# Attention in split halves: three single-pass matmuls for each full-precision f32 matmul of the scores and values

## Chip, cores and metric

One core of a Trainium2 chip runs the whole kernel. The metric is the device time of one execution, the median of three runs. TensorE (PE) multiplies, ScalarE (ACT) and VectorE (DVE) do the elementwise work, SyncE (SP) issues nearly all DMAs.

## What is computed

One layer of a bidirectional encoder over 256 tokens of width 2048: a SwiGLU feed-forward block (5632 wide), a mixing block, a second feed-forward block and a final RMS norm. The mixing block runs a 31-tap depthwise convolution and a latent attention on the same normalised input, gates both with sigmoids and projects the sum. The attention is what the change touches:

```
c_q  = rms_norm(c_q_raw)                      # 768 wide
q    = c_q @ w_uq    -> 16 heads x (128 nope + 64 rope)
c_kv = rms_norm(c_kv_raw)                     # 512 wide
k_nope, v = c_kv @ w_ukv -> 16 heads x (128, 128)
q_rope, k_rope = rotated by the positions     # one k_rope for all heads
s = q_nope . k_nope + q_rope . k_rope
p = softmax(s * 192 ** -0.5)
o = p @ v ;  y_mla = o @ w_o
```

All inputs and outputs are float32.

## The kernel before

**Units.** All weights stream through four slots. A unit is two 128-row blocks of 512 columns (1024 elements a partition), or a smaller one; there are some 814 units, numbered by u over the whole program. SyncE loads unit u into `raw` when VectorE has done with unit u - 4. ScalarE's `round_unit(u)` copies it to `w_hi` as fp32r, once TensorE has used unit u - 4; VectorE's `split_unit(u)` subtracts, `w_lo = raw - w_hi`. The activations are kept in high and low fp32r halves in the same way. `multiply` then makes three single-pass matmuls, high by high, high by low and low by high, into one PSUM bank. ScalarE and VectorE run a loop over u each, four units ahead of TensorE, and whatever else they do stands in that loop at fixed places, so that their order is written out by hand.

**The stages** in order: ffn1 up and down, the convolution's inputs, the latents, the two gates, the rotary queries (`q_rope`), the heads (units H0 = 422 to 453), mla_out (from M0 = 454), conv_out, w_out, ffn2.

**The heads.** Four units for each of eight head pairs s: two of queries (768 elements), one of keys, one of values (1024). `head_pair(s)` on TensorE is: scores of pair s - 1, first query unit (18 matmuls of 256 columns), values of pair s - 2, second query unit (18), keys (24), values' projection (24), then eight 128x128 transposes of the probabilities of pair s - 1 (`attend_turn`). The scores of pair 7 and the values of 6 and 7 stand among the first units of mla_out. Scores and values are matmuls of plain f32 operands, `q_nope`, `k_nope`, `q_rope`, `k_rope`, `probs_t` and `value`.

On ScalarE and VectorE, s is (u - H0) // 4 - 1 and part is (u - H0) % 4. In order within a unit, before the change:
- part 0: ScalarE `attend_exp` of pair s - 1 (waits for the row maximum), the unit, taps, `attend_scale`; VectorE `attend_max`, the unit, taps, `attend_inv`.
- part 1: ScalarE the unit, taps, `attend_out` of pair s - 2 (high half of the head output); VectorE the unit, taps, `keep_queries`, `split_heads`.
- part 2: ScalarE the unit, taps, `keep_keys`; VectorE the unit and taps.
- part 3: ScalarE the unit, taps, `keep_values`, `attend_turn` of pair s - 1 (two copies of turned probabilities); VectorE the unit and taps.

**Taps.** The convolution's 4 x 31 taps, each on four channel blocks, run beside the matmuls. Two of three are four multiplications on ScalarE (`make_tap`, L565) and one addition on VectorE a unit later (`take_tap`, L1185); the third kind is four multiply-adds on VectorE (L1191). `taps_due(u)` says how many are due at unit u: 0.85 a unit up to the rotary queries, after which 110 are done, and then from unit H0 + 4 one a unit until the last 14, which are taps 17 to 30 of the last channel group. `attend_out` of pair 4 waits for the last tap. The convolution's working buffers share memory with the rotary queries and the head outputs; the trace calls all of it q_rope.

**Lines that the prediction speaks of:** L457 `round_unit`, L995 `split_unit`, L565, L1185 and L1191 taps, L572 exponentials, L581 scaling, L588 copies of turned probabilities, L595 and L1218 head outputs, L601 and L607 keys and values, L1212 queries, L1197 row maximum, L1206 reciprocals, L866 and L867 scores, L892 values, L877 transposes, L727 to L729 `multiply`.

Of the kernel before, what the change touches and what calls it, by code (L numbers as in the profile page):

```python
# [14 lines left out]
P = 128  # L15
# [46 lines left out]
class Turn:  # L62


    def __init__(self, hi_before, lo_before, hi, lo):
# [6 lines left out]
         "qrope": (2, 1, 0), "merge": (2, 1, 1)}  # L72
# [6 lines left out]
class Plan:  # L79
    def __init__(self):  # L80
# [14 lines left out]
        self.k_turn = self.more_turns(1, 2, 0)  # L95
# [11 lines left out]
        self.probs_turn = self.more_turns(2 * PAIRS, 1, 0)  # L107
# [56 lines left out]
def encoder(nc, streams, xt_in, x_in, pos_in, gains_in, final_in, taps_in, const_in, freq_in, out):  # L164
# [6 lines left out]
    with ExitStack() as ctx:  # L171
# [10 lines left out]
        h = sb("h", [P, KT, 2, T], F32R)  # L182
# [24 lines left out]
        probs_t = sb("probs_t", [P, 2, 2 * T], F32, outs)  # L207
# [33 lines left out]
        q_rope = sb("q_rope", [P, PAIRS, 4, T], F32, outs)  # L241
        outs.close()
        conv_acc = q_rope[:, 4:8, 1, :]
        conv_prod = (q_rope[:, 4:8, 2, :], q_rope[:, 4:8, 3, :])
# [15 lines left out]
        k_rope = sb("k_rope", [P, 2, T])  # L260
        q_nope = sb("q_nope", [P, 2, T])
        k_nope = sb("k_nope", [P, 2, T])
        value = sb("value", [P, 2, 2, 2 * P])
# [54 lines left out]
        query_step = sem("query_step")  # L318
        q_copied = sem("q_copied")
# [130 lines left out]
        def _(act):  # L450
# [58 lines left out]
            def take_turns(n):  # L509

                g = groups[n]
                for b in range(g.turns):
# [4 lines left out]
                    if g.kind in ("up", "merge"):  # L517
                        dst = hidden if g.kind == "up" else merged
# [8 lines left out]
                    elif g.kind == "qrope":  # L527
                        act.activation(q_rope[:, k:k + 2, 0, :], pair, ACT.Copy).then_inc(turn_hi, 1)

            def take_late_turns():  # L530
# [8 lines left out]
                for j in range(2):  # L539
                    rows = slice(ROPE * j, ROPE * (j + 1))  # L540
                    act.activation(k_rope[rows, j, :], t[rows, 0:T], ACT.Copy).then_inc(turn_hi, 1)
# [54 lines left out]

            def keep_keys(s):
# [40 lines left out]
            for u in range(n_units):  # L638
# [83 lines left out]
        def _(pe):  # L722
# [130 lines left out]
            def attend_scores(p):  # L853
# [3 lines left out]
                pe.wait_ge(turn_hi, turns[g.turn + p % 4 // 2].hi_before + 1)  # L857
# [586 lines left out]
```

## Time and profile before

| | us |
|---|---|
| median of three runs | 2320.63 (2319.89 to 2320.98) |
| the profiled execution, its whole time | 2320.78 |
| its span | 2318.6 |

| engine | busy us | share | instructions |
|---|---|---|---|
| TensorE matmul | 2298.7 | 99% | 10718 |
| TensorE weight load | 1924.2 | 83% | 10718 |
| VectorE | 1322.5 | 57% | 1473 |
| ScalarE | 1188.1 | 51% | 1621 |

The span is what the profiler saw between the first and the last instruction; the execution's own time is 2.2 us more. TensorE's granted clock is 0.999 of full. A matmul row's duration covers a pipelined instruction, so the pace is read from one start to the next. An instruction of ScalarE or VectorE overlaps the next one a little in the same way. L numbers are lines of the kernel before.

### The profile page before, as it was taken

Reading aid. Unit: us, or ns where it says so; the run is one execution under the profiler, and the core shown is the slowest. Engines: PE = TensorE matmul, PEld = TensorE weight load, DVE = VectorE, ACT = ScalarE, POOL = GpSimd, SP = SyncE. Lnnn points to the kernel's source line nnn. Section 1 sums busy time; section 2 is a strip of 40 time slices with the busy share of each in tenths; the row PEclk is TensorE's granted clock in tenths of the full one; section 3 lists DMA queues with packets and bytes.
Section 4 is the critical chain, followed back from the end, with each engine's and each line's share of the span. In section 5 each row is a group of like instructions: output and inputs, shape, how many; then the busy total and the mean of one; then the engine's idle time right before and its main releaser. Section 6 shows DMA issues by size and latency. Waiting matters only on the chain.

```text
span 2318.6 us, 26793 instructions
## 1 busy us (share of the span) xinstructions
PE 2298.7 (99%) x10718; PEld 1924.2 (83%) x10718; DVE 1322.5 (57%) x1473; ACT 1188.1 (51%) x1621; POOL 0.2 (0%) x4
## 2 busy tenths in 40 slices
PE   8999999999999999999999999999999999999998
PEld 7888888888888888878899888888888888888887
DVE  5444544544545488997875465555544554544444
ACT  6444444444444577787776564445444444444443
POOL 0000000000000000000000000000000000000000
PEclk9999999999999999999999999999999999999999
DMA  8666666666666666566643456556666666666664
GB/s 290 190 189 192 189 185 195 190 186 190 192 190 189 191 191 183 180 192 186 200 135 115 139 176 185 183 182 213 190 186 190 190 190 190 190 186 195 192 192 154
DMA packets 121309, 432.65 MB, mean 187 GB/s; under 512 B 13665, under 2 KB 13921, under 8 KB 121057
## 3 DMA queue, kind: packets, MB, share of 16 engines
q1 hardware_dynamic: 121040, 430.51, 60.6%
q8 instruction: 85, 1.39, 0.3%
q10 hardware_dynamic: 144, 0.43, 0.0%
q14 instruction: 40, 0.32, 0.0%
HBM read 428.78 MB, written 2.10 MB: 186 GB/s over the span
## 4 chain that ended last, share of the span: by engine, by line
PE 97%; DVE 1%; ACT 1%; issue 1%; DMA 0%; SPq 0%; ACTq 0%; DVEq 0%
PE bank L727 31%; PE bank L729 31%; PE bank L728 31%; PE turned L738 2%; PE bank L892 1%; PE bank L866 1%; PE bank L867 1%; DVE q_rope L1185 0%; DMA raw<-in_ffn_up 0%; PE turned L877 0%; ACT w_hi L457 0%; DVE w_lo L995 0%; DVE q_rope L1191 0%; PE turned L946 0%; ACT q_rope L565 0%
## 5 line engine op out<-in xcount | busy, mean ns | idle before, releaser
L995 DVE TENSOR_TENSOR w_lo<-raw,w_hi 128x1024 fp32r<-128x1024 f32 (+1 forms) x813 | 985.7, 1215 | 955.2 <-ACT w_hi L457 954.9
L457 ACT ACTIVATE w_hi<-raw 128x1024 fp32r<-128x1024 f32 (+1 forms) x813 | 852.0, 1051 | 997.8 <-PE bank L729 982.4
L727 PE MATMUL bank<-w_hi,h 128*128 128x512 f32 (+1 forms) x2144 | 835.7, 390 | 9.6 <-DVE w_lo L1255 6.4
L729 PE MATMUL bank<-w_hi,h 128*128 128x512 f32 (+1 forms) x2144 | 832.6, 388 | 0.0
L728 PE MATMUL bank<-w_lo,h 128*128 128x512 f32 (+1 forms) x2144 | 832.5, 388 | 0.0
L727 PEld LDWEIGHTS bank<-w_hi,h 128*128 128x128 f32 x2144 | 403.1, 188 | 92.6 <-DVE w_lo L1255 6.4
L729 PEld LDWEIGHTS bank<-w_hi,h 128*128 128x128 f32 x2144 | 402.9, 188 | 82.9
L728 PEld LDWEIGHTS bank<-w_lo,h 128*128 128x128 f32 x2144 | 403.0, 188 | 81.3
L727 PE MATMUL bank<-w_hi,hidden 128*128 128x512 f32 x704 | 274.3, 390 | 0.0
L729 PE MATMUL bank<-w_hi,hidden 128*128 128x512 f32 x704 | 273.9, 389 | 0.0
L728 PE MATMUL bank<-w_lo,hidden 128*128 128x512 f32 x704 | 273.9, 389 | 0.0
L729 PEld LDWEIGHTS bank<-w_hi,hidden 128*128 128x128 f32 x704 | 132.2, 188 | 27.5
L728 PEld LDWEIGHTS bank<-w_lo,hidden 128*128 128x128 f32 x704 | 132.2, 188 | 27.4
L727 PEld LDWEIGHTS bank<-w_hi,hidden 128*128 128x128 f32 x704 | 132.2, 188 | 27.1
L565 ACT ACTIVATE q_rope<-padded,taps 128x256 f32<-128x256 f32 x320 | 135.6, 497 | 1.0 <-DVE q_rope L1185 1.0
L1185 DVE TENSOR_TENSOR q_rope<-q_rope 128x1024 f32<-128x1024 f32 x76 | 92.6, 1218 | 0.0
L1191 DVE SCALAR_TENSOR_TENSOR q_rope<-padded,taps,q_rope 128x256 f32<-128x256 f32 x160 | 66.7, 479 | 0.0
L484 ACT ACTIVATE opened<-bank,rstd 128x512 f32<-128x512 f32 x52 | 32.9, 684 | 37.4 <-PE bank L729 37.4
L727 PE MATMUL bank<-w_hi,attn 128*128 128x512 f32 x128 | 52.0, 406 | 0.0
L727 PE MATMUL bank<-w_hi,merged 128*128 128x512 f32 x128 | 50.2, 392 | 0.0
L729 PE MATMUL bank<-w_hi,attn 128*128 128x512 f32 x128 | 50.1, 391 | 0.0
L728 PE MATMUL bank<-w_lo,attn 128*128 128x512 f32 x128 | 49.9, 390 | 0.0
(184 smaller groups left out, 1226.7 us busy)
## 6 DMA issues: line engine op xcount, KB each, us to landing
raw<-in_ffn_up SPq DMA_DIRECT2D x351, 512.0 KB, 4.1
raw<-in_ffn_down SPq DMA_DIRECT2D x176, 512.0 KB, 3.7
raw<-in_conv_in SPq DMA_DIRECT2D x64, 512.0 KB, 4.1
raw<-in_conv_gate SPq DMA_DIRECT2D x32, 512.0 KB, 4.3
raw<-in_mla_gate SPq DMA_DIRECT2D x32, 512.0 KB, 4.0
raw<-in_mla_out SPq DMA_DIRECT2D x32, 512.0 KB, 3.6
raw<-in_conv_out SPq DMA_DIRECT2D x32, 512.0 KB, 3.6
raw<-in_w_out SPq DMA_DIRECT2D x32, 512.0 KB, 3.6
```

The lines of the kernel that those rows point to most:

```text
L457: act.activation(w_hi[:, j, 0:n], raw[:, j, 0:n], ACT.Copy).then_inc(hi_ready, 1)
L484: act.activation(opened[:, tt, :], banks(g)[tt][:, :], func, scale=rstd[:, tt:tt + 1]).then_inc(by_act, 1)
L565: act.activation(conv_prod[made % 2][:, r, :], padded[:, m, t:t + T], ACT.Copy, scale=taps[:, m, t:t + 1]).then_inc(tap_made, 1)
L727: pe.matmul(dst, fixed_hi, moving_hi, start=first, stop=False)
L728: pe.matmul(dst, fixed_hi, moving_lo, start=False, stop=False)
L729: return pe.matmul(dst, fixed_lo, moving_hi, start=False, stop=last)
L738: last = pe.transpose(turned_bank[n % 2][:, r * T + tt * P:r * T + (tt + 1) * P], src[:, tt, c:c + P], identity[:, :])
L866: pe.matmul(dst, q_nope[:, j, cols], k_nope[:, j, :], start=True, stop=False)
L867: last = pe.matmul(dst, q_rope[:, p, 0, cols], k_rope[:, j, :], start=False, stop=True)
L995: dve.tensor_tensor(w_lo[:, j, 0:n], raw[:, j, 0:n], w_hi[:, j, 0:n], ALU.subtract).then_inc(lo_ready, 1)
L1185: dve.tensor_tensor(dst, conv_acc, conv_prod[made % 2], ALU.add).then_inc(tap_done, 1)
L1191: dve.scalar_tensor_tensor(out=conv_acc[:, r, :], in0=padded[:, m, t:t + T], scalar=taps[:, m, t:t + 1], in1=conv_acc[:, r, :], op0=ALU.mu ...
```

## The change

- `q_nope`, `k_nope`, `q_rope` and `k_rope` get a low half beside the high one and become fp32r; `probs_t` and `value` become fp32r and get `probs_lo` and `value_lo` beside them. The rotary queries and the new low halves lie where `h` lies, which is not in use then.
- Each f32 matmul of scores and values becomes a `multiply` of three fp32r matmuls.
- ScalarE makes all high halves: the query copy moves to it from VectorE (part 1, after `attend_out`).
- VectorE makes the low halves by subtraction: queries (part 1), keys (part 2), values and then the two of the probabilities (part 3), each time after the unit and its tap; also those of the rotary queries and the rotary key in the stages ahead.
- TensorE waits for the low halves (`q_copied`, `k_copied`, `v_copied` and `turn_lo` now count them).
- After unit H0 + 4 the taps are due at 0.65 a unit in place of 1.

```diff
@@ -69,7 +69,7 @@
-         "qrope": (2, 1, 0), "merge": (2, 1, 1)}
+         "qrope": (2, 1, 1), "merge": (2, 1, 1)}
@@ -104,7 +104,7 @@
-        self.probs_turn = self.more_turns(2 * PAIRS, 1, 0)
+        self.probs_turn = self.more_turns(2 * PAIRS, 1, 1)
@@ -385,7 +397,7 @@
         def taps_due(u):
-            n = int(0.85 * max(0, min(u, QR0) - CONV0)) + max(0, u - H0 - 4)
+            n = int(0.85 * max(0, min(u, QR0) - CONV0)) + int(0.65 * max(0, u - H0 - 4))
             open_groups = sum(u >= g.last + 7 for g in plan.stage("conv_in") if g.kind == "glu")
             return min(n, TAPS * open_groups, N_TAPS)
@@ -594,18 +604,23 @@
                 for j in range(2):
                     act.activation(attn[:, 2 * p + j, 0, :], out_bank[:, j * T:(j + 1) * T], ACT.Copy).then_inc(head_hi, 1)
+            def keep_queries(s):
+                act.wait_ge(unit_used, H0 + 4 * s + 2)
+                if s:
+                    act.wait_ge(scores_ready, 2 * s)
+                act.activation(q_nope[:, :, 0, :], q_bank[:, :].rearrange("p (j t) -> p j t", j=2), ACT.Copy).then_inc(q_hi, 1)
+
             def keep_keys(s):
                 act.wait_ge(unit_used, H0 + 4 * s + 3)
                 if s:
                     act.wait_ge(scores_ready, 2 * s)
-                act.activation(k_nope[:, :, :].rearrange("p j t -> p (j t)"), k_bank[:, :], ACT.Copy).then_inc(k_copied, 1)
+                act.activation(k_nope[:, :, 0, :], k_bank[:, :].rearrange("p (j t) -> p j t", j=2), ACT.Copy).then_inc(k_hi, 1)
             def keep_values(s):
                 act.wait_ge(unit_used, H0 + 4 * s + 4)
                 if s > 1:
                     act.wait_ge(value_summed, s - 1)
-                act.activation(value[:, s % 2, :, :].rearrange("p k d -> p (k d)"), v_bank[:, :],
-                               ACT.Copy).then_inc(v_copied, 1)
+                act.activation(value[:, s % 2, :, :].rearrange("p k d -> p (k d)"), v_bank[:, :], ACT.Copy).then_inc(v_hi, 1)
             def fore(n):
                 i, tt = n // 2, n % 2
@@ -681,6 +696,8 @@
                     attend_scale(s - 1)
                 if (s == PAIRS + 1 and part == 0) or (2 <= s <= PAIRS and part == 1):
                     attend_out(s - 2)
+                if part == 1 and 0 <= s < PAIRS:
+                    keep_queries(s)
                 if part == 2 and 0 <= s < PAIRS:
                     keep_keys(s)
                 if part == 3 and 0 <= s < PAIRS:
@@ -854,7 +871,7 @@
                 pe.wait_ge(q_copied, p + 1)
                 pe.wait_ge(k_copied, p + 1)
                 g = plan.stage("q_rope")[p // 4]
-                pe.wait_ge(turn_hi, turns[g.turn + p % 4 // 2].hi_before + 1)
+                pe.wait_ge(turn_lo, turns[g.turn + p % 4 // 2].lo_before + 1)
                 if p:
                     pe.wait_ge(exp_ready, 4 * p)
                 else:
@@ -863,8 +880,10 @@
                     for q in range(2):
                         cols = slice(q * P, (q + 1) * P)
                         dst = scores[j][:, q * T:(q + 1) * T]
-                        pe.matmul(dst, q_nope[:, j, cols], k_nope[:, j, :], start=True, stop=False)
-                        last = pe.matmul(dst, q_rope[:, p, 0, cols], k_rope[:, j, :], start=False, stop=True)
+                        multiply(dst, (q_nope[:, j, 0, cols], q_nope[:, j, 1, cols]),
+                                 (k_nope[:, j, 0, :], k_nope[:, j, 1, :]), True, False)
+                        last = multiply(dst, (q_rope[:, p, 0, cols], q_rope[:, p, 1, cols]),
+                                        (k_rope[:, j, 0, :], k_rope[:, j, 1, :]), False, True)
                     last.then_inc(scores_ready, 1)
             def attend_turn(p):
@@ -886,11 +905,13 @@
                 else:
                     pe.wait_ge(*freed(groups[plan.first_mla - 1]))
                 t = turns[plan.probs_turn + 2 * p + 1]
-                pe.wait_ge(turn_hi, t.hi_before + 1)
+                pe.wait_ge(turn_lo, t.lo_before + 1)
                 for j in range(2):
                     for k in range(2):
-                        last = pe.matmul(out_bank[:, j * T:(j + 1) * T], value[:, p % 2, k, j * P:(j + 1) * P],
-                                         probs_t[:, j, k * T:(k + 1) * T], start=(k == 0), stop=(k == 1))
+                        dims, keys = slice(j * P, (j + 1) * P), slice(k * T, (k + 1) * T)
+                        last = multiply(out_bank[:, j * T:(j + 1) * T],
+                                        (value[:, p % 2, k, dims], value_lo[:, p % 2, k, dims]),
+                                        (probs_t[:, j, keys], probs_lo[:, j, keys]), k == 0, k == 1)
                 last.then_inc(value_summed, 1)
             def block_of(u, k):
@@ -1206,11 +1232,26 @@
                     dve.reciprocal(row_inv[:, j, :], row_sum[:, j, :]).then_inc(inv_ready, 1)
             def keep_queries(s):
-                dve.wait_ge(unit_used, H0 + 4 * s + 2)
-                if s:
-                    dve.wait_ge(scores_ready, 2 * s)
-                dve.tensor_scalar(q_nope[:, :, :].rearrange("p j t -> p (j t)"), q_bank[:, :], 1.0, None,
-                                  ALU.mult).then_inc(q_copied, 1)
+                dve.wait_ge(q_hi, s + 1)
+                dve.tensor_tensor(q_nope[:, :, 1, :], q_bank[:, :].rearrange("p (j t) -> p j t", j=2), q_nope[:, :, 0, :],
+                                  ALU.subtract).then_inc(q_copied, 1)
+
+            def keep_keys(s):
+                dve.wait_ge(k_hi, s + 1)
+                dve.tensor_tensor(k_nope[:, :, 1, :], k_bank[:, :].rearrange("p (j t) -> p j t", j=2), k_nope[:, :, 0, :],
+                                  ALU.subtract).then_inc(k_copied, 1)
+
+            def keep_values(s):
+                dve.wait_ge(v_hi, s + 1)
+                hi, lo = (v[:, s % 2, :, :].rearrange("p k d -> p (k d)") for v in (value, value_lo))
+                dve.tensor_tensor(lo, v_bank[:, :], hi, ALU.subtract).then_inc(v_copied, 1)
+
+            def attend_turn(p):
+                for j in range(2):
+                    n = plan.probs_turn + 2 * p + j
+                    dve.wait_ge(turn_hi, turns[n].hi_before + 1)
+                    dve.tensor_tensor(probs_lo[:, j, :], turned_bank[n % 2][:, :], probs_t[:, j, :],
+                                      ALU.subtract).then_inc(turn_lo, 1)
             def split_heads(p):
                 dve.wait_ge(head_hi, 2 * p + 2)
@@ -1302,6 +1343,12 @@
                     keep_queries(s)
                 if (s == PAIRS + 1 and part == 0) or (2 <= s <= PAIRS and part == 1):
                     split_heads(s - 2)
+                if part == 2 and 0 <= s < PAIRS:
+                    keep_keys(s)
+                if part == 3 and 0 <= s < PAIRS:
+                    keep_values(s)
+                if part == 3 and 1 <= s <= PAIRS:
+                    attend_turn(s - 1)
                 if u == FORE + AHEAD + 8:
                     mean_of_channels()
                 if u == FORE + AHEAD + 11:
...
```

## Rows read from the trace of the kernel before

**Rows 1.** The page, part 1: busy time, share and instructions of each engine.
```profile
PE 2298.7 (99%) x10718; PEld 1924.2 (83%) x10718; DVE 1322.5 (57%) x1473; ACT 1188.1 (51%) x1621; POOL 0.2 (0%) x4
```

**Rows 2.** Stretches, scores to scores: length, busy PE PEld DVE ACT POOL, clock, DMA share, GB/s.
```profile
core 0: us, PE busy (x) PEld busy (x) DVE busy (x) ACT busy (x) POOL busy (x), PEclk, DMA share, GB/s
1184.57:1200.07 15.50, 14.60 (x111) 13.97 (x109) 10.53 (x18) 14.24 (x32) 0.00 (x0) 1.00 0.37 113
1200.07:1218.10 18.03, 16.34 (x117) 15.51 (x117) 13.57 (x25) 14.25 (x35) 0.00 (x0) 1.00 0.36 110
...
1234.44:1250.56 16.12, 16.12 (x118) 15.50 (x117) 8.54 (x15) 10.06 (x23) 0.00 (x0) 1.00 0.40 118
```

**Rows 3.** Timeline of PE, 1215 to 1225: start, us, engine, line, instruction, tiles, shape, idle before.
```profile
1215.38 1.04 PE L877 MATMUL turned<-identity,probs 128*128 128x128 f32 x8
...
1218.10 0.67 PE L866 MATMUL bank<-k_nope,q_nope 128*128 128x256 f32 x2 [1.69 <-issue]
...
1218.61 0.59 PE L867 MATMUL bank<-k_rope,q_rope 128*128 128x256 f32 x2
...
1219.04 0.59 PE L866 MATMUL bank<-k_nope,q_nope 128*128 128x256 f32 x2
...
1221.75 0.28 PE L728 MATMUL bank<-c_q,w_hi 128*128 128x256 f32 x1
...
1221.87 0.28 PE L729 MATMUL bank<-c_q,w_lo 128*128 128x256 f32 x1
...
1223.78 1.89 PE L892 MATMUL bank<-probs_t,value 128*128 128x256 f32 x8
```

**Rows 4.** Timeline of ACT, 1214 to 1229, same columns.
```profile
1214.35 0.63 ACT L595 ACTIVATE attn<-bank 128x256 fp32r<-128x256 f32 x2
...
1214.87 1.05 ACT L457 ACTIVATE w_hi<-raw 128x1024 fp32r<-128x1024 f32 x1
...
1215.83 1.70 ACT L565 ACTIVATE q_rope<-padded,taps 128x256 f32<-128x256 f32 x4
...
1217.42 0.58 ACT L601 ACTIVATE k_nope<-bank 128x512 f32<-128x512 f32 x1
...
1218.84 0.59 ACT L607 ACTIVATE value<-bank 128x512 f32<-128x512 f32 x1
...
1219.32 1.07 ACT L588 ACTIVATE probs_t<-turned 128x512 f32<-128x512 f32 x2
...
1222.18 0.47 ACT L572 ACTIVATE probs<-bank,row_max 128x256 f32<-128x256 f32 x1 [1.79 <-DVE row_max L1200]
...
1224.04 0.84 ACT L457 ACTIVATE w_hi<-raw 128x768 fp32r<-128x768 f32 x1
...
1227.56 1.71 ACT L581 ACTIVATE probs<-probs,row_inv 128x256 f32<-128x256 f32 x4 [1.09 <-DVE row_inv L1206]
```

**Rows 5.** Timeline of DVE, 1215 to 1228, same columns.
```profile
1215.33 0.68 DVE L1212 TENSOR_SCALAR q_nope<-bank 128x512 f32<-128x512 f32 x1
...
1215.93 0.74 DVE L1218 TENSOR_TENSOR attn<-bank,attn 128x256 fp32r<-128x256 f32 x2
...
1216.60 1.21 DVE L995 TENSOR_TENSOR w_lo<-raw,w_hi 128x1024 fp32r<-128x1024 f32 x1
...
1217.73 1.22 DVE L1185 TENSOR_TENSOR q_rope<-q_rope 128x1024 f32<-128x1024 f32 x1
...
1221.26 0.68 DVE L1197 TENSOR_REDUCE row_inv<-bank 128x2 f32<-128x512 f32 x1
...
1225.79 1.67 DVE L1191 SCALAR_TENSOR_TENSOR q_rope<-padded,taps,q_rope 128x256 f32<-128x256 f32 x4
...
1227.37 0.22 DVE L1206 RECIPROCAL row_inv<-row_sum 128x2 f32<-128x2 f32 x2
```

**Rows 6.** Instructions of line L1127: count, ns min/median/max, first and last start, shape.
```profile
L1127 DVE TENSOR_TENSOR hidden<-turned,hidden x44: 679/681/684, 61.3 to 2079.0; 128x512 fp32r<-128x512 f32 x44
```

**Rows 7.** Timeline of PE at the very start of the execution.
```profile
6.42 0.79 PE L727 MATMUL bank<-w_hi,h 128*128 128x512 f32 x1 [6.42 <-DVE w_lo L1255]
...
9.58 0.63 PE L728 MATMUL bank<-w_lo,h 128*128 128x512 f32 x1
```

More of the change, by code:

```diff
@@ L181, in encoder @@
         x = sb("x", [P, 2, D])
-        h = sb("h", [P, KT, 2, T], F32R)
+        outs = ExitStack()
+        h = sb("h", [P, KT, 2, T], F32R, outs)
+        outs.close()
+        outs = ExitStack()
+        q_rope = sb("q_rope", [P, PAIRS, 2, T], F32R, outs)
+        q_nope = sb("q_nope", [P, 2, 2, T], F32R, outs)
+        k_nope = sb("k_nope", [P, 2, 2, T], F32R, outs)
+        probs_lo = sb("probs_lo", [P, 2, 2 * T], F32R, outs)
+        value_lo = sb("value_lo", [P, 2, 2, 2 * P], F32R, outs)
+        outs.close()
+        sb("place_of_h", [P, KT, 2, T], F32R)
         identity = sb("identity", [P, P])
@@ L240, in encoder @@
         outs = ExitStack()
-        q_rope = sb("q_rope", [P, PAIRS, 4, T], F32, outs)
+        scratch = sb("scratch", [P, PAIRS, 4, T], F32, outs)
         outs.close()
-        conv_acc = q_rope[:, 4:8, 1, :]
-        conv_prod = (q_rope[:, 4:8, 2, :], q_rope[:, 4:8, 3, :])
+        conv_acc = scratch[:, 4:8, 1, :]
+        conv_prod = (scratch[:, 4:8, 2, :], scratch[:, 4:8, 3, :])
         merged = sb("merged", [P, KT, 2, T], F32R)
@@ L259, in encoder @@
         c_q = sb("c_q", [P, QT, 2, T], F32R)
[L260 to L263, printed above, removed]
+        k_rope = sb("k_rope", [P, 2, 2, T], F32R)
+        value = sb("value", [P, 2, 2, 2 * P], F32R)
         gain = {}
@@ L318, in encoder @@
         query_step = sem("query_step")
+        q_hi = sem("q_hi")
+        k_hi = sem("k_hi")
+        v_hi = sem("v_hi")
         q_copied = sem("q_copied")
@@ L516, in take_turns @@
                     k = 2 * b + (0 if g.kind in ("kv", "q1") else 4 * g.i)
-                    if g.kind in ("up", "merge"):
-                        dst = hidden if g.kind == "up" else merged
+                    if g.kind in ("up", "merge", "qrope"):
+                        dst = {"up": hidden, "merge": merged, "qrope": q_rope}[g.kind]
                         act.activation(dst[:, k:k + 2, 0, :], pair, ACT.Copy).then_inc(turn_hi, 1)
@@ L540, in take_late_turns @@
                     rows = slice(ROPE * j, ROPE * (j + 1))
-                    act.activation(k_rope[rows, j, :], t[rows, 0:T], ACT.Copy).then_inc(turn_hi, 1)
+                    act.activation(k_rope[rows, j, 0, :], t[rows, 0:T], ACT.Copy).then_inc(turn_hi, 1)
             def make_tap(n):
@@ L1123, in take_turns @@
                     k = 2 * b + (0 if g.kind in ("kv", "q1") else 4 * g.i)
-                    if g.kind in ("up", "merge"):
-                        dst = hidden if g.kind == "up" else merged
+                    if g.kind in ("up", "merge", "qrope"):
+                        dst = {"up": hidden, "merge": merged, "qrope": q_rope}[g.kind]
                         dve.wait_ge(turn_hi, t.hi_before + 1)
@@ L1142, in take_late_turns @@
                                              op1=ALU.subtract).then_inc(turn_lo, 1)
+                dve.wait_ge(turn_hi, turns[plan.k_turn].hi_before + 2)
+                for j in range(2):
+                    rows = slice(ROPE * j, ROPE * (j + 1))
+                    dve.tensor_tensor(k_rope[rows, j, 1, :], turned_bank[plan.k_turn % 2][rows, 0:T], k_rope[rows, j, 0, :],
+                                      ALU.subtract).then_inc(turn_lo, 1)
             def clear_once():
@@ L1208, in keep_queries @@
             def keep_queries(s):
-                dve.wait_ge(unit_used, H0 + 4 * s + 2)
-                if s:
-                    dve.wait_ge(scores_ready, 2 * s)
-                dve.tensor_scalar(q_nope[:, :, :].rearrange("p j t -> p (j t)"), q_bank[:, :], 1.0, None,
-                                  ALU.mult).then_inc(q_copied, 1)
+                dve.wait_ge(q_hi, s + 1)
[10 more added lines that the diff above has]
+            def attend_turn(p):
+                for j in range(2):
+                    n = plan.probs_turn + 2 * p + j
+                    dve.wait_ge(turn_hi, turns[n].hi_before + 1)
+                    dve.tensor_tensor(probs_lo[:, j, :], turned_bank[n % 2][:, :], probs_t[:, j, :],
+                                      ALU.subtract).then_inc(turn_lo, 1)
             def split_heads(p):
```

10 lines of the change are left out of this document (4 added, 6 removed).

## The prediction

> **What bounds the kernel now.** I read the page first [rows 1]: TensorE is busy 99% of the span and is nearly the whole of the chain that ended last, at a full granted clock. So a microsecond taken from its queue is a microsecond of the end, as long as no other engine makes it wait for longer. Then the stretches between one head pair's scores and the next [rows 2], because the change touches only the attention of the eight head pairs. TensorE's own work for a pair is 84 projection matmuls of 256 columns at 0.12 us from start to start, the scores, the values and eight transposes (0.87). A quiet stretch is just that, 16.12 us; the two that carry convolution taps are 15.50 (a pair without values, whose work is 14.41) and 18.03, so they hold stalls of 1.09 and 1.89. Then the three queues in the second of these [rows 3 to 5]: TensorE finishes its transposes at 1216.25 and starts the scores at 1218.10. The page puts that gap down to "issue", but the ScalarE row beside it says what ended it: the copy of k_nope, started at 1217.42 behind a tap of 1.70 us, ended at 1218.00. So in this part of the kernel ScalarE and VectorE already sit at TensorE's heels, and the tap work decides.
>
> **What TensorE saves.** Every f32 matmul shows as two instructions, 0.433 us for the pair (1218.61 to 1219.04, [rows 3]), or 0.216 each. A head pair has 8 such matmuls in the scores (3.46 us) and 4 in the values (1.73 us; the row with x8). Afterwards each is three fp32r matmuls of 256 columns. The nearest rows are the projections around them: same shape, fp32r on both sides, 1221.75 to 1221.87, so 0.12 us each including the weight load. I take it: scores 24 x 0.12 = 2.88, values 12 x 0.12 = 1.44, so 0.87 us less for a pair, 6.95 for eight. TensorE's own work of a stretch becomes 15.27 (13.83 for the first).
>
> **What the two others get.** ScalarE gets a copy of the queries (it takes over the high half that VectorE copied): a 128x512 copy out of a bank, 0.58 us, 0.48 from start to start (1218.84 to 1219.32, [rows 4]). VectorE gives up its query copy (0.60 from start to start, 1215.33 to 1215.93, [rows 5]) and gets five subtractions of 128x512: queries, keys, values and two of probabilities. No such row stands in this stage, but the same form is there elsewhere, 0.681 us each [rows 6]; I take 0.60 as its step, like the copy of the same size, since other 0.68 rows of VectorE follow each other at 0.60. The bounds are 0.55 and 0.67. That is 4 x 0.60 = 2.4 us more for VectorE in a pair. The taps are thinned from 1 to 0.65 for a unit, so the 14 that are left at this point are done over 22 units in place of 14 (taps 17 to 30 of the last channel group): ScalarE makes ten of them (1.60 each), VectorE adds these ten (1.14 each) and makes the other four itself (1.58 each). The tap work itself is not less, and it now reaches into pair 5.
> More important is where the new work stands: the scores now wait for the keys' low half, that is for ScalarE's copy and then VectorE's subtraction, each behind that engine's conversion of the next weight unit, its tap and whatever else its queue holds. And VectorE does the low halves of values and probabilities (0.60 + 1.20) ahead of the row maximum, on which the exponentials wait, with ScalarE's later work behind them.
>
> **The walk.** I went through the three queues in program order, each operation starting when its engine is free and what it waits for has arrived. Steps in us from start to start, all from [rows 3 to 5]: ScalarE conversion 0.96 (128x1024; done at 1.06) and 0.74 (128x768; done at 0.85), tap 1.60, copy 0.48 (done at 0.58), exponential 0.45 with its accumulator read, four scalings 1.62, head copies 0.52; VectorE subtraction of a unit 1.13 or 0.87, tap 1.14 or 1.58, maximum with its scaling 0.80 (the first is through at 0.87), low half 0.60 (done at 0.69), head low halves 0.67, reciprocals 0.2; 0.06 us from a semaphore to the next start, 0.16 from TensorE's next start to its event. Walked through the old program, this starts the scores at 1184.5, 1200.07, 1218.24 and so on to 1298.96, with 3.15 us of stalls; the trace has 1200.07 and 1218.10, and 2.98 of stalls. So it carries the old kernel to within 0.2 us.
> Without taps the new chain from one pair's scores to the next one's is hidden. VectorE reaches the maximum at 2.78 (what is left of the keys' step is -0.15 of overlap, then unit 1.13, values 0.60, probabilities 1.20); first exponential at 3.71, four of them to 5.51; conversion done and seen 0.91, its subtraction 0.87, reciprocals seen 0.28: scaling from 7.57 to 9.19; conversion 0.74, head copies 0.52, queries' high half seen 0.64; the keys' weight unit then waits for TensorE (11.74), its conversion is seen at 12.86, subtracted at 13.99, and the keys' low half is seen at 14.74, before the 15.27 at which TensorE arrives. Half a microsecond is spare, and a tap on either queue costs more than that.
> With taps, the worst stretch (pair 4 to pair 5): the maximum at -0.15 + 1.13 + tap 1.58 + 0.60 + 1.20 = 4.36; first exponential +0.93, exponentials +1.80, conversion +0.91, unit +0.87, tap +1.14, reciprocals +0.28: scaling starts at 10.29; +1.62, conversion +0.74, tap +1.60, head copies +0.52, queries' high half +0.64 = 15.41; VectorE: queries' low +0.60, heads +0.67, unit +1.13, tap +1.14, keys' low +0.75 = 19.70. TensorE's own work is 15.27, so it waits 4.43. In the same way: pair 0 waits 2.03 (VectorE still has the queries' rotary turns and tap 17 ahead of the keys), 0 to 1 is 15.92 against 13.83 (2.09), 1 to 2 is 18.10 (2.83), 2 to 3 is 18.26 (2.99), 3 to 4 is 16.40 (1.13), 5 to 6 is hidden, 6 to 7 is 15.68 (0.41), and the last values wait 0.22. Together 16.1 us of stalls.
>
> **Sum.** Stalls 16.1 - 3.15 = +13.0; TensorE's work -6.95; together +6.0 us. The rest costs nothing: the rotary keys' two low halves (64 rows each) and the larger clearing fall into stages in which TensorE has no stall after them, and the DMAs are at 0.36 to 0.40 of their time in these stretches [rows 2]. The profiled execution took 2320.78 (span 2318.6), 0.15 above the median of 2320.63, so the sum goes on the median: 2326.6. With the low half's step at 0.55 the walk gives +4.5, at 0.67 +8.1; with 0.03 or 0.10 us for a semaphore +5.4 or +6.8.
>
> **Rivals.**
> A, faster: the low halves hide. The two stalls of before came from taps in front of the keys; thinning the taps alone takes the walk's 3.15 to 0.9. If VectorE's subtractions found room, the gain would be 6.95 + 2.3 = 9.2, so 2311.4. The point at which it turns is a stall total of 10.1 us (6.95 + 3.15). For it: VectorE is busy only 8.5 of 16.12 us in a quiet stretch [rows 2]. Against: it is not the load but the order; in the stretch of 18.03 it is busy 13.6, and adding to a queue on whose end TensorE waits can't be free.
> B, no change to be told: the queues run a little closer than my steps and the stalls come to some 12 us: +1.9, so 2322.5. For it: the walk adds eight small overruns of one sign.
> C, the clock: TensorE's rows at the very start stand 0.43 us apart after 6.42 us of idleness, where they are 0.23 later: half pace, the lower of its two levels (1.2 against 2.4 GHz), for the 3.6 us up to 10.0 [rows 7]. The old stalls, at most 1.9 us, were granted 1.00 on both sides. The new one of 4.4 us is longer than any within the old kernel. If the clock falls there once, that costs half of 3.6 us, 1.8: 2328.4; in the three stretches around 3 us too, 2333.8.
> The Trainium skill has this as a rule ("TensorE: Matmul & The Clock Gate", section "HAM oscillation — how this bites in real kernels"): an engine that stands idle between bursts of matmuls falls back to its half rate and starts the next burst cold. The start of this trace agrees; the gaps inside the old kernel don't show it.
> D, the replaced matmuls are not single passes: were they at the 0.216 of the f32 halves, 36 a pair would take 8 x 36 x 0.096 = 28 us more than I reckon, and fill some 8 of the stalls' 16 us: 2346. The projections' rows speak against it.
>
> **How the numbers follow.** Forecast (+4.5 to +8.1) 0.58, A 0.08, B 0.18, C 0.14, D 0.02. About 0.2%, 4.6 us, is what can be told from no change here. Faster is A, 0.08; same is B and the lowest of the forecast's own band, 0.20; slower is the rest, 0.72. The range leaves out A, D and C's upper end: 2321.5 to 2330.5.
>
> **What would show it.** In the trace of after: score matmuls 0.12 us apart; gaps in front of the scores of pairs 0 to 5, the longest at pair 5, each ended by VectorE's subtraction into k_nope; no gap at pair 6; the row maximum behind the probabilities' subtractions; stretches of 15.3 in the quiet end against 18 to 20 with taps; taps that end in pair 5. Wrong it would be if the gaps summed to less than 10 us (A), or if matmuls behind the longest gap stood at double their distance (C). If the keys' low half is not what the scores wait for, the walk has named the wrong chain even where the total fits.

## The result, and the profile after

| | kernel before | changed kernel |
|---|---|---|
| median of seven runs, us | 2320.18 (2319.89 to 2320.98) | 2328.36 (2327.80 to 2330.21) |
| span of the profiled execution, us | 2318.6 | 2326.1 |
| ratio of the times | | 1.0036, 95% interval 1.0027 to 1.0045 |

The changed kernel is 0.36% slower, 8.2 us by the medians and 7.5 by the two spans. Its page, parts 1 and 4 (against [rows 1]):

```profile
PE 2297.4 (99%) x10814; PEld 1925.8 (83%) x10814; DVE 1343.9 (58%) x1511; ACT 1190.8 (51%) x1629; POOL 0.2 (0%) x4
PE 94%; DVE 3%; ACT 2%; issue 1%; DMA 0%; SPq 0%; ACTq 0%
```

TensorE's busy time fell by only 1.3 us, and it lost three points of the chain that ended last (its share fell from 97% to 94%), two of them to VectorE and one to ScalarE. The stretches from one pair's scores to the next one's answer to [rows 2], with the same columns:

```profile
core 0: us, PE busy (x) PEld busy (x) DVE busy (x) ACT busy (x) POOL busy (x), PEclk, DMA share, GB/s
1186.47:1202.38 15.91, 14.06 (x117) 13.86 (x117) 10.46 (x19) 13.38 (x30) 0.00 (x0) 1.00 0.31 109
1202.38:1220.59 18.21, 16.98 (x128) 16.77 (x129) 13.45 (x24) 13.54 (x32) 0.00 (x0) 0.91 0.40 119
1220.59:1238.78 18.19, 15.47 (x128) 15.26 (x129) 13.36 (x24) 13.19 (x32) 0.00 (x0) 1.00 0.32 98
1238.78:1255.02 16.24, 15.48 (x128) 15.28 (x129) 11.78 (x20) 11.30 (x28) 0.00 (x0) 1.00 0.29 100
1255.02:1274.58 19.56, 15.48 (x128) 15.27 (x129) 13.44 (x24) 14.13 (x33) 0.00 (x0) 1.00 0.33 106
1274.58:1291.30 16.72, 16.72 (x129) 16.72 (x129) 9.69 (x17) 8.48 (x20) 0.00 (x0) 0.90 0.40 116
1291.30:1306.98 15.68, 15.49 (x132) 15.28 (x130) 10.13 (x17) 10.95 (x25) 0.00 (x0) 1.00 0.43 133
```

The first number after the stretch is its length, the one behind the comma TensorE's busy time. TensorE's own work is 13.83 in the first and 15.27 in the others. Each stretch is longer than that, four of them by 2 to 4.3 us, and two carry a granted clock of about 0.9. The scores of pair 0 start 1.87 us later than before. The first transpose of the convolution, which closes this part of the program, starts 7.51 later (1333.15 against 1325.64), so the whole change of the span lies in the heads.

Which step ends the longest gap, the one in front of pair 5, is seen when VectorE's and ScalarE's timelines are laid side by side. VectorE, 1255 to 1275, with the idle time before an operation in brackets:

```profile
1255.97 1.67 DVE L1217 SCALAR_TENSOR_TENSOR scratch<-padded,taps,scratch 128x256 f32<-128x256 f32 x4
1257.55 0.68 DVE L1247 TENSOR_TENSOR value_lo<-bank,value 128x512 fp32r<-128x512 f32 x1
1258.15 1.28 DVE L1253 TENSOR_TENSOR probs_lo<-turned,probs_t 128x512 fp32r<-128x512 f32 x2
1259.35 0.68 DVE L1223 TENSOR_REDUCE row_inv<-bank 128x2 f32<-128x512 f32 x1
...
1263.84 1.22 DVE L1211 TENSOR_TENSOR scratch<-scratch 128x1024 f32<-128x1024 f32 x1
1264.97 0.22 DVE L1232 RECIPROCAL row_inv<-row_sum 128x2 f32<-128x2 f32 x2
...
1270.26 0.69 DVE L1236 TENSOR_TENSOR q_nope<-bank,q_nope 128x512 fp32r<-128x512 f32 x1 [1.66 <-ACT q_nope L611]
1270.87 0.74 DVE L1259 TENSOR_TENSOR attn<-bank,attn 128x256 fp32r<-128x256 f32 x2
1271.53 1.21 DVE L1016 TENSOR_TENSOR w_lo<-raw,w_hi 128x1024 fp32r<-128x1024 f32 x1
1272.66 1.22 DVE L1211 TENSOR_TENSOR padded<-scratch 128x1024 f32<-128x1024 f32 x1
1273.80 0.68 DVE L1241 TENSOR_TENSOR k_nope<-bank,k_nope 128x512 fp32r<-128x512 f32 x1
```

ScalarE in the same stretch:

```profile
1265.17 1.71 ACT L591 ACTIVATE probs<-probs,row_inv 128x256 f32<-128x256 f32 x4 [2.24 <-DVE row_inv L1232]
1266.78 0.83 ACT L469 ACTIVATE w_hi<-raw 128x768 fp32r<-128x768 f32 x1
1267.52 1.70 ACT L575 ACTIVATE scratch<-padded,taps 128x256 f32<-128x256 f32 x4
1269.12 0.63 ACT L605 ACTIVATE attn<-bank 128x256 fp32r<-128x256 f32 x2
1269.65 0.58 ACT L611 ACTIVATE q_nope<-bank 128x512 fp32r<-128x512 f32 x1
```

Read in order of time, this is the chain. On VectorE a tap and the low halves of values and probabilities stand ahead of the row maximum (1259.35), and another tap stands ahead of the reciprocals (1264.97). On ScalarE a tap and the head copies stand ahead of the queries' high half (1269.65). On VectorE a weight unit and a tap stand ahead of the keys' low half, which ends at 1274.48. TensorE, which had finished its transposes, starts the scores 0.10 us later:

```profile
1269.47 1.04 PE L896 MATMUL turned<-identity,probs 128*128 128x128 f32 x8
1274.58 0.36 PE L744 MATMUL bank<-k_nope,q_nope 128*128 128x256 f32 x1 [4.08 <-issue]
...
1275.83 0.41 PE L745 MATMUL bank<-k_nope,q_nope 128*128 128x256 f32 x1
1276.05 0.41 PE L746 MATMUL bank<-k_nope,q_nope 128*128 128x256 f32 x1
...
1278.66 0.28 PE L744 MATMUL bank<-k_rope,q_rope 128*128 128x256 f32 x1
1278.78 0.28 PE L745 MATMUL bank<-k_rope,q_rope 128*128 128x256 f32 x1
```

"issue" again stands for a wait that the page can't name; the end of L1241 beside it does. The same distance of 0.10 us lies between the end of L1241 and the scores of pairs 0 to 4 (for pair 1, 1202.28 and 1202.38). And behind this gap the matmuls stand 0.22 us apart (1275.83 to 1276.05), three microseconds later 0.12: TensorE ran at its lower level for a while. The granted clock in 4 us behind the gaps of pairs 1, 3 and 5:

```profile
1202.40:1206.40 4.00, 4.00 (x22) 4.00 (x23) 4.00 (x6) 2.47 (x6) 0.00 (x0) 0.62 0.79 208
1238.78:1242.78 4.00, 4.00 (x33) 4.00 (x34) 3.97 (x7) 0.94 (x3) 0.00 (x0) 1.00 0.57 190
1274.60:1278.60 4.00, 4.00 (x21) 4.00 (x22) 3.57 (x6) 0.36 (x1) 0.00 (x0) 0.57 0.62 200
```

### The profile page after: what moved, and what is told of

Read it like the earlier page. It is cut to its first block, busy times and chain, and to the rows that moved or that the text cites. A ratio compares the mean times of both kernels' runs of the same rounds, so it can differ in the third digit from the quotient of the medians.

```text
span 2326.1 us, 27031 instructions
## 1 busy us (share of the span) xinstructions
PE 2297.4 (99%) x10814; PEld 1925.8 (83%) x10814; DVE 1343.9 (58%) x1511; ACT 1190.8 (51%) x1629; POOL 0.2 (0%) x4
## 4 chain that ended last, share of the span: by engine, by line
PE 94%; DVE 3%; ACT 2%; issue 1%; DMA 0%; SPq 0%; ACTq 0%
PE bank L744 31%; PE bank L745 31%; PE bank L746 31%; PE turned L755 2%; DVE scratch L1211 1%; DVE w_lo L1016 1%; ACT w_hi L469 1%; DVE scratch L1217 0%; ACT scratch L575 0%; ACT probs L582 0%; ACT probs L591 0%; DMA raw<-in_ffn_up 0%; DVE probs_lo L1253 0%; PE turned L967 0%; DVE q_nope L1236 0%
## 5 line engine op out<-in xcount | busy, mean ns | idle before, releaser
L1016 DVE TENSOR_TENSOR w_lo<-raw,w_hi 128x1024 fp32r<-128x1024 f32 (+1 forms) x813 | 985.5, 1215 | 942.0 <-ACT w_hi L469 941.6
L575 ACT ACTIVATE scratch<-padded,taps 128x256 f32<-128x256 f32 x320 | 135.7, 497 | 1.0 <-DVE scratch L1211 1.0
L1211 DVE TENSOR_TENSOR scratch<-scratch 128x1024 f32<-128x1024 f32 x76 | 92.5, 1218 | 0.0
L1217 DVE SCALAR_TENSOR_TENSOR scratch<-padded,taps,scratch 128x256 f32<-128x256 f32 x160 | 66.6, 478 | 0.0
```

The lines of the kernel that those rows point to most:

```text
L575: act.activation(conv_prod[made % 2][:, r, :], padded[:, m, t:t + T], ACT.Copy, scale=taps[:, m, t:t + 1]).then_inc(tap_made, 1)
L1016: dve.tensor_tensor(w_lo[:, j, 0:n], raw[:, j, 0:n], w_hi[:, j, 0:n], ALU.subtract).then_inc(lo_ready, 1)
L1211: dve.tensor_tensor(dst, conv_acc, conv_prod[made % 2], ALU.add).then_inc(tap_done, 1)
L1217: dve.scalar_tensor_tensor(out=conv_acc[:, r, :], in0=padded[:, m, t:t + T], scalar=taps[:, m, t:t + 1], in1=conv_acc[:, r, :], op0=ALU.mu ...
```

## The experiments

The theory on trial: what is lost is the wait for the chain of steps on ScalarE and VectorE between one pair's scores and the next one's; it is the taps in those two queues that push it past TensorE's 15.27 us; and a part of the loss is the clock behind long gaps. The rivals: the low halves cost by themselves, taps or not; ScalarE's added copy or the thinned taps do it; the sum of VectorE's work does it in whatever order.

All times are medians; "before" in the same sessions was 2320.16 to 2320.30. A gap is the time of a stretch less TensorE's own work in it; the idle time in brackets in a timeline is a little shorter (4.08 against a gap of 4.29 at pair 5).

| run | us | ratio to before, 95% interval |
|---|---|---|
| e1 changed, taps early | 2318.13 | 0.9992 (0.9982 to 1.0001) |
| e2 old, taps early | 2322.43 | 1.0011 (1.0002 to 1.0020) |
| e3 old, taps thin | 2318.18 | 0.9991 (0.9981 to 1.0000) |
| e4 changed, gaps filled | 2326.43 | 1.0027 (1.0017 to 1.0038) |
| e5 changed, no low halves | 2313.82 | 0.9973 (0.9962 to 0.9983) |
| e6 changed, f32 matmuls | 2331.75 | 1.0050 (1.0035 to 1.0065) |
| e7 changed, keys first | 2324.74 | 1.0019 (1.0010 to 1.0028) |
| e8 keys first, taps spread | 2315.39 | 0.9979 (0.9970 to 0.9989) |
| e9 keys first, taps eased | 2311.19 | 0.9959 (0.9944 to 0.9973) |
| e10 old, taps eased | 2316.93 | 0.9984 (0.9974 to 0.9993) |
| e11 changed, old tap rate | 2328.01 | 1.0032 (1.0021 to 1.0044) |

### e1 and e2: the taps out of the heads

```diff
-            n = int(0.85 * max(0, min(u, QR0) - CONV0)) + int(0.65 * max(0, u - H0 - 4))
+            n = int(0.85 * max(0, min(u, QR0 - 64) - CONV0)) + int(1.1 * max(0, min(u, QR0) - QR0 + 64))
```

e2 is the same edit in the kernel before.

> The changed kernel with all convolution taps done before the heads: from 64 units ahead of the rotary queries 1.1 taps a unit in place of 0.85, none in the heads. Nothing else differs. Theory (it is the taps in the queues of ScalarE and VectorE that let the new chain overrun TensorE's 15.27 us): gaps in front of the scores fall from some 14 us to about 1.5, a stretch is 15.3 everywhere, the clock stays at full pace, and the time is 8.6 under the kernel before, 2311.6. Rival (the low halves cost by themselves, taps or not): gaps of 1 to 2 us stay in front of most scores, the time stays above 2320. Second rival (the taps' work only moves): the gate stages, where VectorE is busy 31 to 37 of 40 us, get stalls instead; then the heads are as in the theory but the stretch before them is longer by some us.

> The kernel before with the same early taps. Theory: it has only the 3.0 us of stalls to lose, so about 2317.1; together with the run of the changed kernel with early taps this gives what the split halves bring without taps: 5.5 us less (6.95 of matmuls less 1.5 of gaps). Rival (low halves cost by themselves): this kernel is the faster one of the two.

Measured 2318.13 and 2322.43: the split halves now win by 4.3 us, where 5.5 were expected, but they lie 6.5 and 5.3 us above the forecasts (2311.6 and 2317.1). The heads did what the theory said: in e1 the scores are 13.81, then five times 15.25 us apart, with 0.25 us of idle time before pair 0 and 0.18 before pair 7; in e2 they are 14.40 and 16.11 apart. The second rival is right about the rest: the taps moved their price into the gate stages. TensorE's waits between 900 and 1175 in e1 (engine, line, waited for, us in total, times, longest):

```profile
PE bank L744 <- DVE w_lo L1016: 5.5, 5, 2.1
```

The kernel before has 1.9 us in three such waits there, and e2 5.3 in four. That is 3.6 and 3.4 us more. The granted clock explains a further part of what lies over the forecasts. e1, behind an idle time of 2.00 us:

```profile
988.00:992.00 4.00, 4.00 (x11) 3.17 (x12) 3.84 (x12) 3.95 (x8) 0.00 (x0) 0.57 0.45 133
```

Here 43% of 4 us is lost, 1.7 us; in e2 the clock is 0.62 in the 4 us from 1004.32 and 0.95 in the next 4, which is 1.7 too. So in the heads the low halves cost less than 1 us by themselves: from the first scores to the convolution's transposes e1 takes 131.91 us and e2 137.98, which is 6.07 of the matmuls' 6.95. Ahead of the heads they may cost something: pair 0's scores start 1.4 us later in e1 than in e2 (1191.36 and 1189.96), of which TensorE's waits show 0.5; the cause of the rest is open. VectorE has little room there even without the extra taps: in the kernel before it is busy 38.46 of the 40 us from 940 to 980.

### e3 and e11: is it the thinning?

e3 is the kernel before with 0.65 taps a unit in the heads, e11 the changed kernel with 1:

```diff
-            n = int(0.85 * max(0, min(u, QR0) - CONV0)) + max(0, u - H0 - 4)
+            n = int(0.85 * max(0, min(u, QR0) - CONV0)) + int(0.65 * max(0, u - H0 - 4))
```

> The kernel before with the changed kernel's thinning of taps alone (0.65 a unit in place of 1 in the heads). The walk through the queues gives 0.9 us of stalls in place of 3.15, so 2317.9. Rival (thinning is what costs, as it drags the taps out to pair 5): slower than before by some us, with gaps at pairs 3 to 5.

> The changed kernel with the old tap rate in the heads (1 a unit, done in pair 3, in place of 0.65, done in pair 5). Theory (it is the total of tap work between the scores' chains that counts, not how it is spread): the walk gives gaps of 3.2, 3.9, 4.0 and 4.4 us in front of pairs 0 to 3 and 16.1 us in all, the same as for the changed kernel; 5.9 us over the kernel before, 2326.1, and up to 4 more where the clock falls behind three gaps of about 4 us, 2326 to 2330. Rival (thin taps are what makes this change bearable): over 2331.

e3 took 2318.18, against 2317.9 expected: thinning is the good part of the change, worth 2 us in the old kernel, whose one remaining gap is 0.7 us. The interval just reaches 1, but the slowest of e3's ten runs (2319.32) is faster than the fastest of the kernel before (2319.70). e11 took 2328.01, the time of the changed kernel (2328.36) within its spread. Its stretches are 18.53, 19.35 and 19.80 and then 15.24: fewer, longer gaps and the same sum. Both rivals are out. Between these two rates the spread of the taps doesn't matter to the changed kernel, which fits the theory that their total in the chains does.

### e4: the gaps filled

```diff
+                fill = {1: 12, 2: 12, 3: 12, 5: 28}.get(p, 0)
+                if fill:
+                    pe.wait_ge(exp_ready, 4 * p)
+                    for _ in range(fill):
+                        pe.matmul(scores[0][:, 0:T], c_q[:, 0, 0, 0:P], c_q[:, 0, 0, :], start=True, stop=True)
                 pe.wait_ge(q_copied, p + 1)
```

> The changed kernel with idle TensorE time in front of the scores of pairs 1, 2, 3 (12 each) and 5 (28) filled by dummy 256-column fp32r matmuls into the score bank, which the scores then overwrite; nothing waits for longer. Theory (TensorE's clock falls after the long gaps and that costs about 1.5 us behind pair 5's gap): with the engine kept busy the score matmuls all stand 0.12 us apart, the granted clock is 1.00 in each stretch, and the time is about 1.3 us under the changed kernel, 2327.0. Rival (the doubled distance of some 15 matmuls after the gaps has another cause, as the weight unit's transfer or the operands' place): it stays, and the time is that of the changed kernel, 2328.4.

Measured 2326.43, 1.9 us under the changed kernel. TensorE in front of pair 5's scores, and the granted clock behind them:

```profile
1270.83 3.60 PE L875 MATMUL bank<-c_q 128*128 128x256 f32 x28
1275.16 0.35 PE L744 MATMUL bank<-k_nope,q_nope 128*128 128x256 f32 x1 [0.73 <-issue]
...
1276.06 0.28 PE L745 MATMUL bank<-k_nope,q_nope 128*128 128x256 f32 x1
1276.18 0.28 PE L746 MATMUL bank<-k_nope,q_nope 128*128 128x256 f32 x1
```

```profile
1275.00:1279.00 4.00, 3.84 (x32) 3.88 (x33) 3.96 (x8) 0.18 (x1) 0.00 (x0) 1.00 0.69 226
```

The matmuls stand 0.12 apart at a clock of 1.00, and the stretch from pair 5 to pair 6 is 15.22 in place of 16.72. Of the other stretches only pair 1 to pair 2 changed (17.97 against 18.21), so the doubled distance was the clock, and it cost 1.5 us behind pair 5's gap and 0.24 behind pair 1's. From the first scores to the convolution's transposes e4 takes 144.94 us, the changed kernel 146.68, 1.74 more.

### e5 and e6: one part alone

e5 keeps the three matmuls and drops the low halves:

```diff
-                                 (k_nope[:, j, 0, :], k_nope[:, j, 1, :]), True, False)
+                                 (k_nope[:, j, 0, :], k_nope[:, j, 0, :]), True, False)
...
-                                        (value[:, p % 2, k, dims], value_lo[:, p % 2, k, dims]),
+                                        (value[:, p % 2, k, dims], value[:, p % 2, k, dims]),
```

and so on for the other operands. e6 keeps the low halves and their waits and drops the three matmuls:

```diff
-                        multiply(dst, (q_nope[:, j, 0, cols], q_nope[:, j, 1, cols]),
-                                 (k_nope[:, j, 0, :], k_nope[:, j, 1, :]), True, False)
+                        pe.matmul(dst, q_nope[:, j, 0, cols].bitcast(F32), k_nope[:, j, 0, :].bitcast(F32), start=True, stop=False)
```

> The changed kernel without the low halves of queries, keys, values and probabilities: the three matmuls stay, with the high half in the low one's place, and TensorE waits for the high halves alone. This leaves out the attention's low-order terms and VectorE's subtractions. Theory (the loss is the wait for the low halves' chain): the walk gives 2.6 us of gaps in place of some 14 and 7.5 us less than the kernel before, 2312.7. Rival (ScalarE's added query copy and the thinned taps are what makes the scores late): the gaps stay near those of the changed kernel and the time above 2325.

> The changed kernel with all its low halves made and waited for, but one f32 matmul of the high halves in the place of the three (the low-order terms of the attention are left out). TensorE then does the old 0.87 us a pair more. Theory: part of that lies in gaps that are there anyway, so not 6.95 but 3.4 us more than the changed kernel's walk: 9.4 us over the kernel before, 2329.6, and up to 1.5 more where the clock falls behind the long gap, 2331. Rival (TensorE is the bound in all stretches): 6.95 over the changed kernel, 2335.3.

e5 took 2313.82 (expected 2312.7), 6.4 us less than before with the taps still in the heads. One gap of size is left, 1.8 us in front of pair 1 (two more are 0.3 and 0.4); a quiet stretch is 15.23. So ScalarE's query copy and the taps alone cost little, and the low halves' chain with the taps costs 2328.36 - 2313.82 = 14.5 us, the clock's share included. e6 took 2331.75 (expected 2329.6 to 2331), 3.4 us over the changed kernel where TensorE does 6.95 us more: half of the matmuls' saving falls into gaps and is worth nothing. TensorE still idles 3.38 us in front of its pair 5.

### e7: another order of the same work

```diff
                 if part == 0 and 1 <= s <= PAIRS:
                     attend_exp(s - 1)
+                if part == 2 and 0 <= s < PAIRS:
+                    keep_keys(s)
...
-                if part == 2 and 0 <= s < PAIRS:
-                    keep_keys(s)
                 if part == 3 and 0 <= s < PAIRS:
                     keep_values(s)
```

on ScalarE, and likewise on VectorE.

> The changed kernel with the keys' high and low halves put ahead of the next weight unit and of the tap on ScalarE and VectorE; no other order changes. Theory (the order in the queues decides): the gap in front of pair 0 goes, the others shrink to 1 to 2.7 us, small gaps of up to 1.7 us come in front of the values; the walk gives 13.1 us in all in place of 16.1, 3.0 us less than the changed kernel's walk, and with no gap over 2.7 us the clock should stay up at pair 5: 2323 to 2325. Rival (VectorE has too much work in all, order or not): as the changed kernel, 2328.4.

Measured 2324.74, in the range. Pair 0 starts at 1185.29 (before the edit 1186.47), and the clock is 1.00 behind its gaps. New small gaps stand where the walk had put them, in front of the values (`probs_t`), beside those that are left in front of the scores:

```profile
1217.86 0.36 PE L744 MATMUL bank<-k_nope,q_nope 128*128 128x256 f32 x1 [0.69 <-issue]
1224.69 0.35 PE L744 MATMUL bank<-probs_t,value 128*128 128x256 f32 x1 [1.56 <-DVE probs_lo L1253]
1236.05 0.36 PE L744 MATMUL bank<-k_nope,q_nope 128*128 128x256 f32 x1 [0.93 <-issue]
```

The same operations in another order cost 3.6 us less, so the sum of VectorE's work alone is not the cause. Of the 3.6, 1.3 is the stretch from pair 5 to pair 6 (15.45 in place of 16.72), which is the clock. But the order alone doesn't save the change.

### e8 to e10: a version that beats both

e8 is e7 with this tap schedule, and e9 with the next one; e10 is the kernel before with e9's.

```diff
+            n = int(1.05 * max(0, min(u, QR0 - 88) - CONV0) + 0.5 * max(0, min(u - QR0 + 88, 24)) + 1.07 * max(0, min(u, QR0) - QR0 + 64))
```

```diff
+            n = int(1.1 * max(0, min(u, QR0 - 88) - CONV0) + 0.4 * max(0, min(u - QR0 + 88, 24)) + 0.75 * max(0, min(u - QR0 + 64, 14)) + 1.06 * max(0, min(u, QR0 + 5) - QR0 + 50))
```

> The changed kernel with the keys' halves first as in the run before, and all taps before the heads, but spread by VectorE's load: 1.05 a unit in the convolution's input stage, 0.5 in the latents, 1.07 in the gates. Theory: no gaps in the heads but 0.2 us, 9.9 us less than the kernel before (2310.3) if the earlier stages take the taps without new stalls; the first try with early taps had 5.5 us of stalls between 950 and 1170, against 1.9 before, so with the lighter load in the latents something between 2310 and 2314. Rival (VectorE is too full before the heads however the taps are spread): 2317 to 2318, as with the first early taps.

> As the run with the keys first and spread taps, but the taps are eased where its profile showed the stalls: 1.1 a unit in the convolution's input stage, 0.4 in the latents, 0.75 for the first 14 gate units (in which VectorE also normalises the queries), then 1.06 up to one unit before the last rotary one. Theory: no gaps in the heads; the four gaps of 4.1 us between 980 and 1005 shrink to what the old kernel has there, 1.9 us; so about 2 us less than the 2315.4, 2313 to 2314. Rival (those gaps come from the late queries' own chain, and the taps before it don't matter): 2315 to 2316.

> The kernel before with the same eased taps. Theory: the same gaps before the heads, none in the heads, but f32 matmuls: 6.95 us more than the run of the changed kernel with keys first and eased taps, since without taps the matmuls' saving arrives whole. Rival (the split halves keep a price of their own): the difference is under 5 us.

e8 took 2315.39, above its 2310 to 2314: no gap in the heads, but 4.1 us of gaps just before 1004, one of them 2.07 us. e9 took 2311.19, some 2 us better than its forecast of 2313 to 2314: three gaps are left there, 1.6 us together (before: 1.9). The forecast had left out the clock. Behind e8's gap of 2.07 us it is 0.67 for 4 us and 0.90 for the next 4, a loss of 1.7, and in e9 it is 1.00. With the 2.5 us of gaps this makes the whole 4.2 us between e8 and e9.

```profile
986.44 0.50 PE L744 MATMUL bank<-w_hi,h 128*128 128x512 f32 x1 [0.22 <-DVE w_lo L1016]
989.78 0.50 PE L744 MATMUL bank<-w_hi,h 128*128 128x512 f32 x1 [0.28 <-DVE w_lo L1016]
1008.47 0.50 PE L744 MATMUL bank<-w_hi,h 128*128 128x512 f32 x1 [1.11 <-DVE w_lo L1016]
```

Two stretches of e9's heads:

```profile
1185.04:1198.79 13.75, 13.75 (x118) 13.75 (x117) 7.86 (x14) 10.37 (x21) 0.00 (x0) 1.00 0.40 138
1198.79:1214.04 15.25, 15.25 (x131) 15.25 (x130) 9.68 (x17) 10.18 (x24) 0.00 (x0) 1.00 0.39 121
```

and the same two of e10:

```profile
1185.02:1199.42 14.40, 14.40 (x111) 13.98 (x110) 6.73 (x11) 10.32 (x20) 0.00 (x0) 1.00 0.42 131
1199.42:1215.53 16.11, 16.11 (x118) 15.49 (x117) 7.49 (x13) 10.05 (x23) 0.00 (x0) 1.00 0.36 114
```

Length and busy time agree in all four, so nothing waits in them and what differs is the matmuls alone: 0.65 and 0.86 us a stretch. e10 took 2316.93, 5.7 us more than e9 by the medians and 6.6 by the spans (2316.0 and 2309.4); 6.95 was expected. About 0.4 of it is missing in the last stretch, where e9's lead is 0.70 for the last scores and two values in place of 0.58 + 2 x 0.29 = 1.16; the walk has the last values wait 0.22 there for the low halves of the probabilities.

e9 is 9.1 us under the kernel before (ratio 0.9959) and 17 under the changed one, with the same operations as the latter.

## Why the prediction was right, and where it was off

**The sign and the size.** Forecast +6.0 us with 2321.5 to 2330.5, measured +8.2 (2328.36). The walk through the three queues was the right tool. Its stretches, added up, put the scores of pairs 0 to 7 at 1186.6, 1202.5, 1220.6, 1238.8, 1255.2, 1274.9, 1290.2 and 1305.9; the trace has 1186.47, 1202.38, 1220.59, 1238.78, 1255.02, 1274.58, 1291.30 and 1306.98. Up to pair 5 no start is off by more than 0.4 us.

**TensorE's saving.** Each fp32r matmul took 0.12 us, as [rows 3] said, which was to save 0.87 us a pair; e9 against e10 shows 0.86 in a quiet stretch. In the changed kernel about half of it fell into gaps (e6). **VectorE's low halves**, 0.60 from start to start by analogy with [rows 5] and [rows 6], are 0.61 in the trace (1270.26 to 1270.87), and the instruction is 0.69 long. **The chain**: the order of steps named for pair 4 to 5 is the one in the two timelines above, the forecast 19.70 against 19.56.

**The gaps.** Forecast 16.1 us, of which 2.03, 2.09, 2.83, 2.99, 1.13 and 4.43 in front of pairs 0 to 5. The trace: 1.87, 2.08, 2.94, 2.92, 0.97 and 4.29, then 1.45 for the stretch to pair 6, where none was forecast, and 0.41 to pair 7, as forecast. That is 16.9 us, of which 15.5 were set by the other engines' chains and 1.45 by TensorE's own slower pace.

**Rival C came in on top**, at 0.14 in the forecast. By the prediction's own list this was a sign of being wrong: the matmuls behind the longest gap stand at double their distance. The 1.45 us behind pair 5's gap is the clock, priced at 1.8 from the start of the trace [rows 7]; e4 gave it back. The walk left it out of the sum, and that is the mis-sized term: 6.0 + 1.45 = 7.5, the difference of the spans. The range held the result because it was wide enough to take in rival C's lower end; that C's single number, 2328.4, is the measured median is partly luck, as its 1.8 was one fall and the trace has 1.50 and 0.24 for two. The clock fell behind pair 1's gap too (0.62), but there it cost only those 0.24 on the path, since the stretch to pair 2 ends with ScalarE's and VectorE's chain; the rest came out of the gap in front of pair 2, whose idle part is only 1.24 us. What was wrong in rival C was the condition: it expected the long gap first and three of about 3 us next, and the trace has it at 4.1 and at 1.8 us of idle time but not at 2.7. Its source was thinner than it looked, too. The rows at the start of the execution show half the pace, but the clock column for the same time (6.42 to 10.00) says 1.00, so there the lower level was read from the pace alone; behind pair 5's gap the column and the pace agree.

The Trainium skill's rule on this ("TensorE: Matmul & The Clock Gate", section "HAM oscillation — how this bites in real kernels") is that idle time between bursts sends TensorE to its half rate. The 0.57 behind pair 5's gap agrees; behind the 2.72 us of idle time in front of pair 3 the clock stayed at 1.00.

**Rival A**, the hidden low halves, needed gaps of less than 10 us in all; they were 17. e1 and e9 show that its reason was sound, only its condition wasn't met: with the taps gone the chain is hidden, as the walk's 14.74 against 15.27 said. Thinning the taps alone was worth 2.0 us (e3), 2.3 in the walk.

**What stays open.** With the clock's share the sum meets the difference of the spans within 0.2 us; the 0.7 us by which the medians differ more than the spans is within the runs' spread. Whether the taps could be moved to VectorE's and ScalarE's idle time after the heads wasn't tried, because the head outputs of pairs 4 to 7 share their memory.

## What to carry to other kernels

When matmuls are made cheaper by work on other engines, write down the chain from one use of the result to the next and compare its length, in queue order, with TensorE's own time; busy shares don't show it (VectorE was busy 13.44 of the 19.56 us in the worst stretch). Put what TensorE waits for ahead of what nobody waits for, and move filler work (here taps) to where the chain is slack before adding to the chain. Then look at the stage that takes the filler: here it brought some 3.5 us of gaps and 1.7 us of slower clock, until it was spread by VectorE's load.

## What the runs showed of the hardware

An idle TensorE fell to half pace behind gaps much shorter than the prediction had supposed, and not every time. The table has the granted clock in the 4 us behind a gap, by the idle time of TensorE that the timeline shows in front of it.

| idle, us | run: granted clock |
|---|---|
| 1.69 | before: 1.00 |
| 1.84 | e6, twice: 1.00; changed kernel: 0.62 |
| 2.00 | e1: 0.57; e2: 1.00 |
| 2.07 | e1: 1.00; e2: 0.62; e8: 0.67 |
| 2.18 and 2.27 | e7: 1.00 |
| 2.32 and 2.38 | e11: 0.69 and 0.65 |
| 2.72 | changed kernel: 1.00 |
| 3.38 | e6: 0.57 |
| 4.08 | changed kernel: 0.57 |

In e11, after 2.97 and after 2.83:

```profile
1206.18:1210.18 4.00, 4.00 (x21) 4.00 (x22) 4.00 (x6) 1.35 (x3) 0.00 (x0) 0.57 0.50 160
1245.33:1249.33 4.00, 4.00 (x33) 4.00 (x34) 3.96 (x7) 0.34 (x1) 0.00 (x0) 1.00 0.66 221
```

Two gaps of nearly the same length, one with the fall and one without. The length of the gap alone doesn't decide; what does is not shown. In the changed kernel a fall nearly doubled the distance of some 15 matmuls of 256 columns (0.21 us in place of 0.12). It cost 1.45 to 1.5 us behind pair 5's gap, where TensorE set the end, and 1.76 with the f32 matmuls of e6 (17.87 us to pair 6 in place of 16.11).
